# A two-block transformer kernel: part of the second block's output projection, two copies and the rotation are put at other places around its attention

## The reference

```python
p = xn @ w_in[l]                       # xn: normalised, scaled and shifted x
q = apply_rope(q_heads(p[..., OFF_Q:OFF_K], q_norm_g[l]), cos, sin)
k = apply_rope(k, cos, sin)
attn = attend_query_blocks(q, concat([kc, k]), concat([vc, v]))   # 4 heads of 64, 512 keys
# the four mixers, 256 columns each
four = fft2(u_f).real @ w_fourier
conv = silu(layer_norm(depthwise31(glu) + dw_b)) @ w_conv_pw
pool = (windowed_mean(u_p) - u_p) @ w_pool * pool_scale
x = x + gate1 * (concat([attn, four, conv, pool]) @ w_out)        # 1024 x 1024
x = x + gate2 * swiglu(norm(x) ..., w_ffn_in, w_ffn_out)          # 1024 -> 2816 -> 1024
```

## Time and profile before

| what | us |
|---|---|
| median of 3 runs | 2664.6 (2658.77 to 2665.36) |
| the profiled execution, its own time | 2667.12 |
| its span | 2665.2 |
| PE busy / DVE busy / ACT busy / POOL busy | 2488.0 / 1471.6 / 938.9 / 593.7 |
| mean granted clock of TensorE | 0.984 of full |

### The profile page before, as it was taken

One profiled execution on the slowest core, in us unless ns is written; L12 is line 12 of the kernel. 1 busy time (PEld: TensorE's weight loads), 2 busy tenths in 40 slices (PEclk: granted clock), 3 DMA queues, 4 the chain that ended last, 5 costly groups with the idle time before them and its releaser, 6 DMA issues.

```text
span 2665.2 us, 29500 instructions
## 1 busy us (share of the span) xinstructions
PE 2488.0 (93%) x9800; PEld 1693.8 (64%) x9800; DVE 1471.6 (55%) x3162; ACT 938.9 (35%) x2319; POOL 593.7 (22%) x600
## 2 busy tenths in 40 slices
PE   8999999988888979999998899999898999999999
PEld 6568655433444546677555555567366888868888
DVE  3623686889777637324877777778656200172000
ACT  2351354435544322432444435432456100161000
POOL 0000333333344410002333333443422000030000
PEclk9999999999999999999999999999999999999999
DMA  7475999999999994558999999999982444424444
GB/s 279 174 278 181 411 423 427 421 397 409 389 427 427 420 383 153 218 216 321 404 427 426 426 427 409 427 426 421 425 321 79 144 156 156 160 79 143 155 146 157
DMA packets 113647, 817.47 MB, mean 307 GB/s; under 512 B 12432, under 2 KB 14528, under 8 KB 14944
## 3 DMA queue, kind: packets, MB, share of 16 engines
q0 software_dynamic: 75136, 549.29, 49.4%
q1 hardware_dynamic: 38368, 266.35, 27.0%
HBM read 814.54 MB, written 1.05 MB: 306 GB/s over the span
## 4 chain that ended last, share of the span: by engine, by line
PE 56%; DMA 22%; DVE 14%; ACT 3%; issue 3%; POOL 1%; ACTq 0%; DVEq 0%; SPq 0%; POOLq 0%
PE work L669 41%; DMA arena<-experts,arena 22%; PE acc L669 14%; DVE arena L2027 4%; DVE arena L1816 3%; POOL arena L635 1%; PE work L761 1%; DVE small L1816 1%; ACT L1491 1%; DVE arena L1975 1%; DVE arena L1976 1%; DVE arena L1978 1%; ACT arena L1501 1%; DVE arena L1977 0%; DVE arena L1974 0%
## 5 line engine op out<-in xcount | busy, mean ns | idle before, releaser
L669 PE MATMUL acc<-arena 128*128 128x512 f32 (+1 forms) x1900 | 885.7, 615 | 127.9 <-ACT arena L1501 125.6
L669 PE MATMUL work<-arena,ring 128*128 128x256 f32 (+2 forms) x3524 | 768.3, 379 | 4.5 <-DVE arena L2211 2.0
L669 PEld LDWEIGHTS work<-arena,ring 128*128 128x128 f32 x3524 | 667.2, 191 | 110.0 <-issue 14.0
L635 POOL DMA_INDIRECT arena<-experts,arena x512 | 530.4, 1036 | 894.6 <-PE acc L669 717.3
L669 PEld LDWEIGHTS acc<-arena 128*128 128x128 f32 (+1 forms) x1900 | 357.6, 195 | 559.3 <-issue 356.3
L2027 DVE SCALAR_TENSOR_TENSOR arena<-arena,h 128x1024 f32<-128x1024 f32 x256 | 311.6, 1225 | 177.3 <-DMA arena<-experts,arena 174.2
L2027 DVE SCALAR_TENSOR_TENSOR arena<-arena,acc 128x1024 f32<-128x1024 f32 x256 | 308.0, 1220 | 152.4 <-DMA arena<-experts,arena 148.6
L669 PE MATMUL work<-h,ring 128*128 128x256 f32 (+1 forms) x1440 | 323.4, 377 | 3.3 <-DMA ring<-stream 1.5
L669 PEld LDWEIGHTS work<-h,ring 128*128 128x128 f32 x1440 | 264.9, 190 | 70.6 <-issue 36.5
L1491 ACT ACTIVATE arena<-arena 128x2 f32<-128x2 f32 x258 | 52.4, 203 | 616.6 <-DVE arena L2027 615.7
L669 PE MATMUL work<-lent,ring 128*128 128x256 f32 x992 | 224.2, 379 | 0.0
(11 more groups left out here) (262 smaller groups left out, 1833.4 us busy)
## 6 DMA issues: line engine op xcount, KB each, us to landing
ring<-stream SPq DMA_DIRECT2D x252, 1024.0 KB, 5.0
arena<-experts,arena POOLq DMA_INDIRECT x512, 12.4
arena<-na_bias POOLq DMA_DIRECT2D x2, 2048.0 KB, 15.4
arena<-consts POOLq DMA_DIRECT2D x1, 2304.0 KB, 13.4
lent<-consts POOLq DMA_DIRECT2D x2, 1024.0 KB, 8.4
arena<-consts POOLq DMA_DIRECT2D x1, 1816.0 KB, 18.6
x<-x_in SPq DMA_DIRECT2D x1, 1024.0 KB, 5.5
xc<-ctx_in POOLq DMA_DIRECT2D x1, 1024.0 KB, 11.3
```

The costliest lines, as they stand in the source:

```text
L635: pool.indirect_dma_start(rows[:, m % ROWS, :], None, experts[l], bass.IndirectOffsetOnAxis(ap=expert[:, n:n + 1], axis=0))\
L669: ins = nc.tensor.matmul(o, w, r, start=start, stop=stop, **kw)
```

## The change

Per layer of the second block, in both layers:

- **Output tiles beside the attention.** The first four of the eight output tiles (`OUT_BESIDE = 4`) no longer go through the `work` banks. They are summed in the four `acc` banks, 256 columns each, in parts: slices 2 and 3 of `mix` (8 matmuls) at G1 of pair 2, slice 6 (4 matmuls) at G0 of pair 3, slice 7 (4) at G1 of pair 3, slices 0 and 1 (8) behind `pw`, slices 4 and 5 (8) behind the copies of `pw`. The first part waits until all 8 exponentials have been taken. The other four tiles follow as before. The stream of weights is reordered to match. VectorE adds these tiles from `acc` on the semaphore `out_beside`.
- **Copies by VectorE.** The copies of `four` and `plin` move from ScalarE's `mix_after_turn(1)` and `(2)` to VectorE's `mix_after_pair(1)` and `(2)`.
- **Rotation ahead of the last taps.** VectorE runs 6 of the 9 remaining taps, then the rotation, then the last 3 (`TAPS_LAST`).
- **Second `pool` item.** It moves from ahead of the attention to G1 of pair 0, and ScalarE's copy of it to `mix_after_turn(0)`.

```diff
-MIX_BEFORE = ("dft", "dft", "pool", "pool")
-MIX_BETWEEN = {("G0", 0): ("dft",), ("G0", 1): ("mean",), ("G1", 1): ("four", "four"), ("G0", 2): ("var",),
+TAPS_LAST = 3
+MIX_BEFORE = ("dft", "dft", "pool")
+OUT_BESIDE = 4
+OUT_BEFORE_PW, OUT_AFTER_PW = {("G1", 2): (2, 3), ("G0", 3): (6,), ("G1", 3): (7,)}, ((0, 1), (4, 5))
+MIX_BETWEEN = {("G0", 0): ("dft",), ("G1", 0): ("pool",), ("G0", 1): ("mean",), ("G1", 1): ("four", "four"), ("G0", 2): ("var",),
...
+                def out_beside(ks, first=False, last=False):
+                    for n in range(OUT_BESIDE):
+                        for k in ks:
+                            mm(acc[:, n * 512:n * 512 + T], tile(), mix[:, k, :], first and k == ks[0],
+                               last and k == ks[-1], inc=sem("out_beside") if last and k == ks[-1] else None)
+                            read()
+
+                pooled(0)
+
                 def mix_between(kind, p):
-                    if (kind, p) == ("G0", 0):
+                    if (kind, p) == ("G1", 0):
+                        pooled(1)
+                    elif (kind, p) == ("G0", 0):
...
+                        copied(pe, f"four{l}", 1)
+                        pe.wait_ge(sem(f"attx{l}_exp"), 4 * TT)
+                        out_beside((2, 3), first=True)
+                    elif kind[0] == "G" and p == 3:
+                        copied(pe, f"plin{l}", 1)
+                        out_beside((6,) if kind == "G0" else (7,))
...
+                copied(pe, f"attx{l}O", 4 * TT - 1)
+                out_beside((0, 1))
                 copied(pe, f"pw{l}", 1)
-                for n in range(KD):
+                out_beside((4, 5), last=True)
+                for n in range(KD - OUT_BESIDE):
...
-                for _ in taps:
-                    pass
+                for _ in range(CONV - TAPS_FIRST - TAPS_LAST):
+                    next(taps)
                 V.need("c2_rest", 16)
...
                     V.step(v.tensor_tensor(q, q, wide(rtmp2), ALU.add), f"rotated2_{l}")
+                for _ in taps:
+                    pass
...
                     elif p == 1:
+                        for n in range(2):
+                            b = V.full(f"four{l}", n)
+                            V.free(v.tensor_copy(mix[:, 2 + n, :], b[:, 0:T]), f"four{l}", n)
                         b = V.full(f"var{l}")
                         V.free(v.tensor_copy(rnorm2, b[:, 0:T]), f"var{l}")
                     elif p == 2:
+                        for g in range(2):
+                            b = V.full(f"plin{l}", g)
+                            V.free(v.tensor_scalar(mix[:, 6 + g, :], b[:, 0:T], k2("pool_scale", l)[:, g:g + 1], None,
+                                                   ALU.mult), f"plin{l}", g)
```

More of the change, by code:

```diff
@@ L282, in item_table @@
         attention(f"attx{l}", 8, layer=l)
-        for name, n in (("pw", 2), ("out2_", 8), ("ffn", 1), ("fnorm2_", 1),
+        for name, n in (("pw", 2), ("out2_", KD - OUT_BESIDE), ("ffn", 1), ("fnorm2_", 1),
                         ("ffn", 2 * KF - 1), ("ffo", 8)):
@@ L1281, in _, with pooled @@
                 pm = k2("pool")
-                for c in range(2):
+                def pooled(c):
                     b = bank(f"pool{l}", c)
@@ L1757, in _, with pool_out @@
                     A.free(f(ab[:, t, :], b[:, :], ACT.Copy), f"dft{l}", t)
-                for g in range(2):
+                def pool_out(g):
                     b = A.full(f"pool{l}", g)
@@ L1761, in _ @@
                     A.free(f(zp[HD:P, g, :], b[HD:P, T:2 * T], ACT.Copy), f"pool{l}", g)
+                pool_out(0)
                 def mix_after_exp(u):
@@ L1768, in mix_after_turn @@
                 def mix_after_turn(p):
-                    if p == 1:
+                    if p == 0:
+                        pool_out(1)
+                    elif p == 1:
                         copied(act, f"mean{l}", 0)
@@ L1772, in mix_after_turn @@
                             A.step(f(csq[:, g, :], cv[:, g, :], ACT.Square), "csq")
-                        for n in range(2):
-                            b = A.full(f"four{l}", n)
-                            A.free(f(mix[:, 2 + n, :], b[:, 0:T], ACT.Copy), f"four{l}", n)
                     elif p == 2:
@@ L1778, in mix_after_turn @@
                         A.step(f(rnorm2, rnorm2, ACT.Sqrt, bias=k1("eps")), "var_root")
[L1779 to L1782, removed]
                     elif p == 3:
@@ L1793, in _ @@
                 for k in range(KD):
-                    copied(act, f"out2_{l}", k)
+                    if k < OUT_BESIDE:
+                        A.need("out_beside_added", l * OUT_BESIDE + k + 1)
+                    else:
+                        copied(act, f"out2_{l}", k - OUT_BESIDE)
                     A.step(f(h2[:, k, :], x1[:, k, :], ACT.Square), f"sqf2_{l}", last=False)
@@ L2295, in _, with add_gated @@
                 attention(f"attx{l}", units2(), prob2, mix_after_pair)
-                def add_gated(item, chunk, gs=None, squares=None):
+                def add_gated(item, chunk, gs=None, squares=None, early=0):
                     for n in range(KD):
-                        b = V.full(item, n)
                         o = x1[:, n, :]
-                        V.free(stt(o, b[:, 0:T], mod[:, chunk * KD + n, 1:2], o, ALU.mult, ALU.add), item, n)
+                        if n < early:
+                            V.need("out_beside", l * early + n + 1)
+                            V.step(stt(o, acc[:, n * 512:n * 512 + T], mod[:, chunk * KD + n, 1:2], o, ALU.mult, ALU.add),
+                                   "out_beside_added")
+                        else:
+                            b = V.full(item, n - early)
+                            V.free(stt(o, b[:, 0:T], mod[:, chunk * KD + n, 1:2], o, ALU.mult, ALU.add), item, n - early)
                         if squares:
@@ L2307, in _ @@
                 shift_column(3)
-                add_gated(f"out2_{l}", 2, gs2, f"sqf2_{l}")
+                add_gated(f"out2_{l}", 2, gs2, f"sqf2_{l}", OUT_BESIDE)
                 normalise_tokens(f"fnorm2_{l}", 2 * l + 2, f"hsf2_{l}")
@@ L2353, in align, with put_mixers @@
             parts.append(np.zeros((-n % BT, P, P), np.float32))
-    def put_mixers(l, order):
+    def put_mixers(l, order, out_beside=0):
         w = a["w_in_2"][l]
@@ L2369, in put_mixers @@
         parts.append(bd)
+        t = tiles_of(a["w_out_2"][l][head_columns(0, ATT2_ORDER) + list(range(256, D))], "n").reshape(KD, KD, P, P)
+        if out_beside:
+            for ks in OUT_BEFORE_PW.values():
+                parts.append(t[:out_beside, list(ks)].reshape(-1, P, P))
         put(a["w_conv_pw_2"][l])
-        put(a["w_out_2"][l][head_columns(0, ATT2_ORDER) + list(range(256, D))])
+        if out_beside:
+            for ks in OUT_AFTER_PW:
+                parts.append(t[:out_beside, list(ks)].reshape(-1, P, P))
+        parts.append(t[out_beside:].reshape(-1, P, P))
     def put_ffn(l):
@@ L2420, in stream_parts @@
     for l in range(DEPTH):
-        put_mixers(l, TOKEN_FM)
+        put_mixers(l, TOKEN_FM, OUT_BESIDE)
         put_ffn(l)
```

## The result

The changed kernel takes 2646.98 us (median of 4 runs, 2643.86 to 2649.45), the kernel before 2664.91 (2658.77 to 2665.36, 4 runs): 0.993 of the time, 95% interval 0.9917 to 0.9943, so 17.9 us less. The forecast was 2645.4, 19.2 us less.

The account below looks back on a forecast made before the run. TensorE, busy 93%, was taken as the bound, though it waits for ScalarE in the attention. Gains of 8.7 us (layer 0) and 10.5 (layer 1), together 19.2, took the median 2664.6 to 2645.4 us; range 2639 to 2655.

Parts of the forecast that it names:

- The earlier start: Attention start: rotation ahead of three taps and later second `pool` item bring the first maximum 2.24 us earlier, what follows 1.9.
- Copies by VectorE at nothing: `four` and `plin` copies fit VectorE's idle 1.80 and 2.40 us, so moving them there costs nothing.
- Sixteen matmuls without a wait from `plin` to the last O: Inserted attention matmuls run without TensorE waits; `pw` starts 0.8 us later than before, with 6.9 us more work behind it.
- Behind `pw`: Output projection: 52 matmuls, 22.4 us, and 0.43 to the last add, 8.7 us earlier than before in layer 0.
- The clock: TensorE's clock stays at 2.4 GHz (granted 1.00) from scores to FFN; layer 1 regains 1.83 us more than layer 0.
- the rival: TensorE's clock falls all the same despite dense work: 8.7 us lost, gain 10.5, time 2654; chance 0.09.
- The sum: Both layers of the second block: 8.7 us in layer 0 and 10.5 in layer 1, together 19.2.
- clock and bubble: Part of the gain, at `pw`: the low clock and TensorE's wait there removed, 7 us.
- the rest: Remaining part of the gain, from TensorE's filled waits in the attention: 8.7 us.
- The chain carried: Rival in the attention: 16 matmuls add their whole 6.9 us to the chain; gain 10.8, time 2654; chance 0.08.

Follow-up runs that it names:

- the filler: Changed kernel with OUT_BESIDE = 0 and 8 + 4 + 4 unread identity matmuls at the inserted places: 2662.5 us, 0.9994 of the kernel before.
- the start alone: Changed kernel with nothing inserted and copies on ScalarE, leaving the earlier rotation and moved `pool` item: one run of 2667.54 us.
- eight inside: Changed kernel with only slices 2 and 3 (8 matmuls per layer) inside the attention, slices 6 and 7 behind `pw`: one run of 2654.89 us.

## Why the prediction was right, point by point

- *The earlier start.* Forecast 2.24 us for the first maximum, measured 2.25 in both layers, and by the forecast parts: cheap taps of 0.51 us behind the rotation, and the first score ready 0.32 us ahead of its maximum, for 0.2 (2023.53 and the 1.23 us from a score to its maximum, against 2025.08). The second `pool` item does delay the first O, without a wait, and by a little more than forecast: it takes 1.92 us up to the weights of the O (2031.47 to 2033.39), for 1.72, and `plin` comes 1.76 us earlier in layer 0, for 1.9.
- *Copies by VectorE at nothing.* Right for layer 0, by the run with the copies back on ScalarE. The two `plin` copies, which had no row before, take 1.00 us together (L2322), at the upper bound of 0.8 to 1.0. In layer 1 the move cost about 0.3 us, see the next point.
- *Sixteen matmuls without a wait from `plin` to the last O.* Right: `plin` to last O as in the steps, and one wait of 0.73 us left where 0.7 was forecast. `pw` was forecast 0.8 us later than before and to take under 1.9 us; it is 0.96 later in layer 0 and 1.24 in layer 1, and its row has 1.99 us. In layer 1 VectorE waits 0.71 us for the first exponential where in layer 0 it waits 0.43; ScalarE's table load for the exponentials starts 0.36 us behind the maximum's end there (2358.61, after a row that ends at 2358.25), and 0.08 in layer 0. The 0.28 is most of the shortfall of that layer (10.09 for 10.5). Measured from the first maximum, the load stands 0.27 to 0.29 us later in layer 1 than in layer 0 in all six kernels whose copies of `four` and `plin` are on VectorE, and the same to 0.01 in the three that have them on ScalarE, the kernel before among them. So it comes with the move of the copies, a cost that the forecast did not have; how, stays open. The first table load for the exponentials in layers 0 and 1 of the changed kernel:

```profile
2026.03 1.28 ACT L1399 ACT_TABLE_LOAD   x1 [2.20 <-DVE neg_mx L1851]
2358.61 1.28 ACT L1399 ACT_TABLE_LOAD   x1 [2.48 <-DVE neg_mx L1851]
```

- *Behind `pw`.* 22.82 us to the last add in both layers, by the forecast 22.8.
- *The clock.* At 1.00 throughout, and the layers are alike; that the activity does it, not the content, is shown by the filler. The term was read from one execution, though, and that it came out is in part luck: where the clock falls without the insertion moves between executions, so the 1.83 us by which layer 1 was longer is a sample (1.40 with nothing inserted, 2.19 with the start alone). What does not move is how long it stays low: 6.8 us in layer 0 and 10.2 us in layer 1 in all three traces without the insertion, by windows of half a microsecond. The prediction's 10.60 us for layer 1 is a little too long: its window has a mean of 0.52, not 0.50. And its reason against the rival, that the clock fell only behind three waits in a row, does not hold: two were enough in the run with the start alone.
- *The sum.* 18.6 us between the reciprocals and the last adds, for 19.2; 17.9 by the medians. By the forecast's parts: the earlier start is 3.2 at `plin` for 3.5, clock and bubble from the start of `pw` on are 7.0 for 7, and the rest is 8.4 for 8.7.
- *The rivals.* The clock did not fall again in any trace with matmuls put into the waits. The Trainium skill (TensorE: Matmul & The Clock Gate, "A second HAM failure mode: psum-queue depth-cycling") says that short pauses between groups of matmuls can make the clock swing. The three traces without the insertion fit it; with eight inside, TensorE paused 1.04 and 1.36 us behind dense work at a clock of 1.00. The chain carried nearly half of the 16 matmuls (`pw` 3.2 us later than with nothing inserted, for 6.9 us of them), which the forecast's steps had counted as the later `pw`.

Where the 18.6 us come from, by the runs: with nothing inserted, start and copies give 2.5; the insertion gives 7.5 and 8.6, the difference between the changed kernel and that run. Of each of these 6.9 are the matmuls and 0.8 the covered copies of `pw`, so that the later `pw` (3.2 us against that run) and the clock that stays up cancel to within a microsecond.

## What to carry to other kernels

Work of a dense stage can be put into the waits of a thin stage ahead of it, if a free accumulator and its operands are there; where the filled engine then becomes the bound, each further microsecond put in pushes the chain behind it, and nearly half of the 16 matmuls here did. Count the clock as a part of such a gap: it was low for 6.8 or 10.2 us behind two or three waits of 0.9 to 1.9 us, in part over work that needed no waiting, and it stayed up once the waits were filled. And an edit that takes load off an engine (the copies here) can be worth nothing once another engine sets the pace in the same stage.

## What the runs showed of the hardware

A VectorE tap with both operands in SBUF takes 0.84 us while GpSimd adds its own taps and 0.5 when it has ended; in the changed kernel the first six still take 0.84 on average (the row of 5.87 us for 7 holds them and a product of the head norm) and the three behind the rotation 0.51. The windows of these two stretches show GpSimd (the fifth busy time) at work in the first, 4.54 of 5.30 us, and not in the second:

```profile
2014.70:2020.00 5.30, 5.30 (x21) 3.61 (x20) 5.05 (x8) 0.55 (x2) 4.54 (x6) 1.00 0.07 9
2023.50:2025.05 1.55, 1.52 (x8) 0.69 (x8) 1.46 (x3) 0.33 (x1) 0.00 (x0) 1.00 0.86 354
```

This agrees with the Trainium skill (SBUF — State Buffer, "Who interferes with whom"), by which a VectorE instruction with two SBUF inputs contends with a GpSimd instruction that reads SBUF. The 32 useless matmuls were as good as free, where they had been expected to cost 2 us (2661 for 2659): the run with the filler takes the same time as the run without. Of their 6.9 us per layer 3.7 lie in waits, and the clock that they keep up gives back 3.0 and 4.1 us for the other 3.2.
